# Interleaving the value matmuls of two attention branches in opposite column halves of TensorE

## What is computed

```
w    = softmax(where(key <= query, q k^T * scale, -inf));        o_mla = w v
z    = sq sk^T * scale;  log_1m = where(key < query, log_sigmoid(-z), 0)
a    = where(key < query, exp(log_sigmoid(z) + suffix_sum(log_1m)), 0);   o_sb = a sv
merged = g_mla * (o_mla @ w_branch_mla) + g_sb * (o_sb @ w_branch_sb)
```

## Time and profile before

| | |
|---|---|
| median of 3 runs | 2427.37 us (2427.21 to 2428.22) |
| profiled execution | 2424.88 us, span 2423.6 us, mean granted clock of TensorE 0.976 |
| TensorE busy | 2349.8 us, 97% of the span |
| VectorE busy | 839.4 us, 35% |
| ScalarE busy | 448.4 us, 19% |
| GpSimd busy | 1287.7 us, 53% |
| attention loop | about 1770 to 1902 us after the span's start |

### The profile page before, as it was taken

The page is one execution under the profiler, slowest core; times in us unless marked ns, Lnnn a source line. Parts: engine busy times, 40 slices in busy tenths (PEclk is TensorE's granted clock), DMA queues, the critical chain, the costliest instruction groups (busy, mean ns, idle before and its releaser), DMA issues.

```text
span 2423.6 us, 26205 instructions
## 1 busy us (share of the span) xinstructions
PE 2349.8 (97%) x11108; PEld 1938.4 (80%) x11108; DVE 839.4 (35%) x910; ACT 448.4 (19%) x712; POOL 1287.7 (53%) x734
## 2 busy tenths in 40 slices
PE   7999999999989999999999999999899999999999
PEld 6888888787768888888888888778667788888887
DVE  2323103666444333203232202430568733333013
ACT  2111003222313111003111102011257221111012
POOL 4666665754015666665666665666100456666654
PEclk9999999999679999999999999999899999999999
DMA  4333332221002333332333332233100222333322
GB/s 155 97 99 100 96 96 78 81 76 61 9 27 87 96 96 96 96 97 77 96 97 100 99 96 80 87 96 98 35 1 1 62 91 92 96 96 96 106 87 86
DMA packets 55580, 201.06 MB, mean 83 GB/s; under 512 B 6408, under 2 KB 6536, under 8 KB 55336
## 3 DMA queue, kind: packets, MB, share of 16 engines
q1 hardware_dynamic: 53712, 193.62, 25.8%
q10 hardware_dynamic: 1752, 5.77, 0.6%
HBM read 197.27 MB, written 2.10 MB: 82 GB/s over the span
## 4 chain that ended last, share of the span: by engine, by line
PE 69%; DVE 4%; ACT 1%; issue 1%; POOL 0%; DMA 0%; DVEq 0%; POOLq 0%; ACTq 0%
PE psum L340 13%; PE psum L341 13%; PE psum L342 13%; PE psum L402 6%; PE psum L400 6%; PE psum L401 6%; PE psum L478 2%; PE psum L813 1%; PE psum L821 1%; PE psum L850 1%; PE psum L592 1%; PE psum L438 1%; PE psum L959 1%; PE psum L960 1%; PE psum L961 1%
## 5 line engine op out<-in xcount | busy, mean ns | idle before, releaser
L322 POOL TENSOR_SCALAR w_hi<-w_raw 128x1024 fp32r<-128x1024 f32 (+1 forms) x365 | 396.6, 1087 | 1089.0 <-PE psum L342 583.6
L324 POOL TENSOR_TENSOR w_lo<-w_raw,w_hi 128x1024 fp32r<-128x1024 f32 (+1 forms) x365 | 891.7, 2443 | 30.5
L340 PE MATMUL psum<-u_hi,w_hi 128*128 128x512 f32 (+1 forms) x2072 | 791.3, 382 | 11.1 <-DVE work L1527 4.0
L341 PE MATMUL psum<-u_hi,w_lo 128*128 128x512 f32 (+1 forms) x2072 | 787.5, 380 | 0.0
L342 PE MATMUL psum<-u_lo,w_hi 128*128 128x512 f32 (+1 forms) x2072 | 787.0, 380 | 0.0
L340 PEld LDWEIGHTS psum<-u_hi,w_hi 128*128 128x128 f32 x2072 | 390.7, 189 | 87.9 <-DVE work L1527 4.5
L342 PEld LDWEIGHTS psum<-u_lo,w_hi 128*128 128x128 f32 x2072 | 390.7, 189 | 74.2
L341 PEld LDWEIGHTS psum<-u_hi,w_lo 128*128 128x128 f32 x2072 | 390.7, 189 | 73.1 <-issue 0.5
L400 PE MATMUL psum<-w_hi,hidden_hi 128*128 128x512 f32 x768 | 298.8, 389 | 0.0
L401 PE MATMUL psum<-w_lo,hidden_hi 128*128 128x512 f32 x768 | 298.8, 389 | 0.0
L402 PE MATMUL psum<-w_hi,hidden_lo 128*128 128x512 f32 x768 | 298.8, 389 | 0.0
(11 more groups left out here) (261 smaller groups left out, 1776.7 us busy)
## 6 DMA issues: line engine op xcount, KB each, us to landing
w_raw<-in_ffn_in SPq DMA_DIRECT2D x176, 512.0 KB, 3.5
w_raw<-in_ffn_out SPq DMA_DIRECT2D x88, 512.0 KB, 3.5
w_raw<-in_proj_in SPq DMA_DIRECT2D x34, 512.0 KB, 3.5
w_raw<-in_mix_in SPq DMA_DIRECT2D x29, 512.0 KB, 3.4
w_raw<-in_embed SPq DMA_DIRECT2D x10, 512.0 KB, 3.5
w_raw<-in_mix_out SPq DMA_DIRECT2D x8, 512.0 KB, 3.5
w_raw<-in_branch SPq DMA_DIRECT2D x8, 512.0 KB, 3.6
w_raw<-in_proj_out SPq DMA_DIRECT2D x8, 512.0 KB, 3.5
```

Source lines behind the costliest of these rows:

```text
L322: pool.tensor_scalar(hi, raw, 1.0, 1.0, ALU.mult, ALU.mult).then_inc(k.w_split, 1)
L324: pool.tensor_tensor(lo, raw, hi.bitcast(F32), ALU.subtract).then_inc(k.w_split, 1)
L340: pe.matmul(out, hi[:, cols], xhi, start=first, stop=False)
L341: pe.matmul(out, lo[:, cols], xhi, start=False, stop=False)
```

## The change

The two value steps become one function, values(h, m), which issues for each of the seven causal blocks the stick branch's matmul of head h and then the softmax branch's matmul of head m. It is called with m = h-1 relative to its stick head, so the two write opposite halves of the array's columns. In step h of TensorE's loop this is values(h-1, h-2); step 1 has the stick branch alone, and after the loop come values(7, 6) and values(None, 7).

So that head h-1's transposed probabilities can lie while those of h-2 are read, turned writes to one of two buffers by the head's parity; the odd one is in two pieces, so odd heads have two copies (1024 and 256 columns) where there was one. On VectorE mla_out(h-2) now stands behind stick_out(h-1) and ahead of softplus(h); mla_out(h-1) behind softplus(h) is gone. After the loop it runs mla_out(6) and mla_out(7) behind stick_out(7). maxima waits for the first query block's logits and, ahead of the second reduction, for the rest. The pairs are made at other steps, and the merge's first product takes the stick branch's four inputs first.

```
+        self.turned = [[(0, N_CAUSAL, turned)], [(0, 2 * T, k.big[:, 4 * T:6 * T]), (2 * T, N_CAUSAL, k.diag[:, 0:N_CAUSAL - 2 * T])]]
-COMPLETE = {1: [0], 3: [1], 4: [4], 5: [2, 5], 6: [6], 7: [3, 7]}
+COMPLETE = {3: [0], 4: [4], 5: [1, 5], 6: [6], 7: [2], 8: [7, 3]}
 pe_attend, logits:
-        m.then_inc(k.logits_done, 1)
+            if i in (ROWS[0][0], ROWS[-1][0]):
+                m.then_inc(k.logits_done, 1)
 pe_attend, values (in place of stick_values and mla_values):
+    def values(h, m):
+        if h is not None:
+            pe.wait_ge(k.z_weights, h + 1)
+            if h:
+                pe.wait_ge(k.z_out, h)
+        if m is not None:
+            pe.wait_ge(k.p_copied, m + 1)
+            if m:
+                pe.wait_ge(k.o_out, m)
+            else:
+                pe.wait_ge(k.norm_var, NORM["heads"])
+        last = len(CAUSAL_BLOCKS) - 1
+        for n, (i, t0, width, c) in enumerate(CAUSAL_BLOCKS):
+            if h is not None:
+                v = H.sv[...]
+                z = pe.matmul(k.ps[7][half(h), t0:t0 + width], v, H.z[h % 2][:, c:c + width], ...)
+            if m is not None:
+                v = H.v[...]
+                o = pe.matmul(k.ps[6][half(m), t0:t0 + width], v, H.turned_at(m, c, width), ...)
+        if h is not None:
+            z.then_inc(k.z_values, 1)
+        if m is not None:
+            o.then_inc(k.o_values, 1)
 pe_attend, loop and end:
-            stick_values(h - 1)
-            mla_values(h - 1)
+            values(h - 1, h - 2 if h > 1 else None)
...
-    stick_values(AH - 1)
-    mla_values(AH - 1)
+    values(AH - 1, AH - 2)
+    values(None, AH - 1)
 pe_merge:
-        for part in range(2):
+        for part in (1, 0):
 act_attend and dve_attend: pairs(h - 1) becomes pairs(h); ScalarE's waits for both outputs become
+            if n < 4:
+                act.wait_ge(k.o_out, 2 * n + 2)
+            else:
+                act.wait_ge(k.z_out, 2 * n - 6)
 dve_attend, maxima:
-        dve.wait_ge(k.logits_done, h + 1)
-        for i, c in ROWS:
+        dve.wait_ge(k.logits_done, 2 * h + 1)
+        for n, (i, c) in enumerate(ROWS):
+            if n == 1:
+                dve.wait_ge(k.logits_done, 2 * h + 2)
 dve_attend, turned:
-        if h:
-            dve.wait_ge(k.o_values, h)
-        dve.tensor_copy(H.turned, k.psum[:, B0:B0 + N_CAUSAL]).then_inc(k.p_copied, 1)
+        if h >= 2:
+            dve.wait_ge(k.o_values, h - 1)
+        for a, b, x in H.turned[h % 2]:
+            d = dve.tensor_copy(x[:, 0:b - a], k.psum[:, B0 + a:B0 + b])
+        d.then_inc(k.p_copied, 1)
 dve_attend, loop and end:
             stick_out(h - 1)
+            if h > 1:
+                mla_out(h - 2)
         softplus(h)
-        if h:
-            mla_out(h - 1)
...
     stick_out(AH - 1)
+    mla_out(AH - 2)
     mla_out(AH - 1)
```

More of the change, by code:

```diff
@@ L781, in __init__ @@
         self.sq, self.sk = [tile(k.big, 6 + n) for n in range(4)], [tile(k.big, 10 + n) for n in range(4)]
-        self.probs, self.turned, *self.z = (row(k.big[:, (KF + LATENT_AT) * T:], n) for n in range(4))
+        self.probs, turned, *self.z = (row(k.big[:, (KF + LATENT_AT) * T:], n) for n in range(4))
+        self.turned = [[(0, N_CAUSAL, turned)], [(0, 2 * T, k.big[:, 4 * T:6 * T]), (2 * T, N_CAUSAL, k.diag[:, 0:N_CAUSAL - 2 * T])]]
         self.soft = [row(k.scf, n) for n in range(2)]
@@ L794, in __init__, with turned_at @@
         self.o = self.sk + self.sq
-COMPLETE = {1: [0], 3: [1], 4: [4], 5: [2, 5], 6: [6], 7: [3, 7]}
+    def turned_at(self, h, c, n):
+        return next(x[:, c - a:c - a + n] for a, b, x in self.turned[h % 2] if a <= c and c + n <= b)
+COMPLETE = {3: [0], 4: [4], 5: [1, 5], 6: [6], 7: [2], 8: [7, 3]}
 PAIRS = [n for h in sorted(COMPLETE) for n in COMPLETE[h]]
+CAUSAL_BLOCKS = sorted(CAUSAL, key=lambda x: (x[0], x[1]))
 def pe_attend(k):
@@ L861, in transpose @@
         m.then_inc(k.p_turned, 1)
-    def stick_values(h):
-        pe.wait_ge(k.z_weights, h + 1)
-        if h:
[L866 to L871, removed]
-        if h:
[L873 to L877, removed]
+    def values(h, m):
[12 more added lines that the diff above has]
+            if h is not None:
+                v = H.sv[:, ((h // 2) * NT + i) * P + h % 2 * HV:((h // 2) * NT + i) * P + (h % 2 + 1) * HV]
+                z = pe.matmul(k.ps[7][half(h), t0:t0 + width], v, H.z[h % 2][:, c:c + width], start=n == 0, stop=n == last, skip_group_check=True)
+            if m is not None:
+                v = H.v[:, (m * NT + i) * HV:(m * NT + i + 1) * HV]
+                o = pe.matmul(k.ps[6][half(m), t0:t0 + width], v, H.turned_at(m, c, width), start=n == 0, stop=n == last, skip_group_check=True)
+        if h is not None:
+            z.then_inc(k.z_values, 1)
+        if m is not None:
+            o.then_inc(k.o_values, 1)
     def spread_key(h):
@@ L1341, in pairs @@
         for n in COMPLETE.get(h, ()):
-            act.wait_ge(k.o_out, h + 1)
-            act.wait_ge(k.z_out, h + 1)
+            if n < 4:
+                act.wait_ge(k.o_out, 2 * n + 2)
+            else:
+                act.wait_ge(k.z_out, 2 * n - 6)
             act.copy(tile(k.uhi, n), H.o[n]).then_inc(k.pair_hi, 1)
@@ L1358, in act_attend @@
         act.copy(H.soft_hi, s).then_inc(k.soft_hi, 1)
-        pairs(h - 1)
+        pairs(h)
     weigh(AH - 1)
-    pairs(AH - 1)
+    pairs(AH)
 def act_embed(k):
@@ L1976, in dve_attend @@
             stick_out(h - 1)
+            if h > 1:
+                mla_out(h - 2)
         softplus(h)
-        if h:
-            mla_out(h - 1)
-        else:
+        if h == 0:
             for n in range(1, AH):
```

## The result

The changed kernel takes 2444.6 us (median of 4 runs, 2443.19 to 2450.55) against 2427.29 of the kernel before: ratio 1.0079, interval 1.0059 to 1.0100. The forecast was slower by 6.8 us, 2434.2, with a range to 2446. The direction and the ring were right; the size was not: 17.3 us. That 2444.6 lies inside the range is luck: the range's upper part was kept for column halves that overlap badly (rival 1), and they overlap fully.

A forecast was written before the change was run, and what follows sets the result against it. TensorE's queue was taken as the bound, with a ring through VectorE and ScalarE 0.2 us under it. Six rings 3.4 - step 1's 0.1 + tail 1.4 + 7d, d = 0.3, gave +6.8 on 2427.37: 2434.2 us, range 2428 to 2446.

The forecast's parts named there:

- the ring: Attention loop, split to split through mask matmul, logits, transposes, values, stick_out, softplus and cast: 13.43 us without TensorE's own queue.
- rival 1: Paired values: column halves overlap badly, d from 0.5 to 2.2 us, making the kernel 9.3 to 20.1 us slower; chance 0.24.
- TensorE's queue and the ring lie 0.2 us apart: Attention loop: TensorE's queue repeats every 13.64 us, the ring takes 13.43, so freeing TensorE alone gives at most about 0.2.
- mla_out's slot: VectorE, between stick_out and softplus: the copy's new place adds 0.72 us to the ring in each head.
- Ring after, 14.15 + d: Split to split in steps 2 to 7 after the change: 14.2 + d on average against 13.64, six rings costing 3.4 + 6d.
- Step 1, 13.5 against 13.64: Loop's first step, without softmax half or mla_out: 13.5 us against 13.64, a gain of 0.1 us.
- d = 0.3: Paired values: d is the delay of the last stick pass, hence of stick_out; taken as 0.3 us, ends 0 and 2.2.
- Early maxima worth nothing: VectorE's first maxima reduction, about 0.7 us, moves earlier, but stick_out still waits for the values: counted as zero.
- Tail 1.4 + d, stall gone: Last split to merge: 11.0 + d against 9.6 us, 1.4 + d longer, with the merge's 0.38 us stall gone.
- Rival 4: TensorE's clock falls after the new waits; a fall over one head would make about +10 us; chance 0.02.

The follow-up runs named there:

- e3_busy: The changed kernel with mla_out moved back behind softplus and matmuls of constants in TensorE's waits: 2425.91 us, ratio 1.0002 to the kernel before.
- e6_unpaired_act: The kernel before, values unpaired, with the first maxima reduction ahead of the remaining logits and stick_out moved to ScalarE: 2422.3 us, ratio 0.9982.
- e8_busy_loop: The changed kernel with matmuls of constants in TensorE's waits ahead of the sums alone: 2431.13 us, ratio 1.0021 to the kernel before.
- experiment 4: The changed kernel with mla_out moved back behind softplus: 2438.8 us, ratio 1.0052; with matmuls of constants in TensorE's waits too, 2425.91 us, ratio 1.0002.
- experiment 5: The kernel before with only the first maxima reduction run ahead of the wait for the remaining logits: 2426.46 us, ratio 0.9999.
- e1_busy: The changed kernel with matmuls of constants ahead of the sums and of the last transposes and last seven value blocks: 2431.88 us, ratio 1.0026.

## Why the prediction was wrong in size

- *TensorE's queue and the ring lie 0.2 us apart; freeing TensorE alone gives nothing*: right in what it gives. e3_busy, which has the pairing without mla_out's slot and with TensorE kept busy, is 1.0002 times the kernel before. The 13.64 us are not TensorE's work alone, though: TensorE's row of weight loads shows that in the kernel before the softmax values wait 0.2 us for the copy turned, which the merged row of 28 passes hides.

```profile
1859.56 0.41 PEld L478 LDWEIGHTS psum<-work 128*64 128x64 f32 x4 [0.21 <-DVE work L1929]
```

  So 28 passes in one half after the other take 4.48 us, not 4.67, and in e6_unpaired_act, where that wait is gone, the queue repeats every 13.47 to 13.48 us.
- *Ring after, 14.15 + d*: right, 14.13 to 14.38 where the clock held (e8_busy_loop). *Step 1, 13.5 against 13.64*: wrong by little; the first two splits are 14.84 us apart before and 14.83 after, so there was no 0.1 to gain.
- *d = 0.3*: too high; it is 0. Column halves in alternation lose nothing, where the row halves of the earlier trace rows, changed every eight passes, reached 80%. That took 2.1 us from the sum. The estimate of d = 0.5 from the figure in the Trainium skill's page "TensorE: Matmul & The Clock Gate", Part 3, was too high in the same way. That part also says that tiles of the array work on several matmuls at once; the trace agrees, with starts 0.00 to 0.01 us apart.
- *mla_out's slot, 0.72 a head*: right (experiment 4). *Early maxima worth nothing*: right (experiment 5). *Tail 1.4 + d, stall gone*: right, 1.5.
- *Rival 4, the clock: "with waits of 1.94 and less it stays at 1.00 ... so it stays"*: this is the step that failed. It put the cost of the new waits at nothing. In six of the seven heads I had their lengths nearly right: up to 0.6 us on the exponents and 1.9 on the cast were forecast, and the trace has 0.50 and 1.31 to 2.17. The last head's I had wrong: "the longest I expect is some 2 us", and it is 5.12, since the 1.94 us of the earlier trace rows and the new slack add up there. From one wait of 1.94 us, behind 96 us in which TensorE had no pause (1793 to 1889 us), I concluded that any number of such waits is free. The trace of the kernel before spoke against that already: at the start of the attention loop the clock fell within a microsecond of a wait of 0.52 us (the row behind the wait, then two windows with the granted clock).

```profile
1770.15 3.90 PE L813 MATMUL psum<-work 64*128 64x128 f32 x14 [0.52 <-DVE work L1882]
...
1769.00:1771.00 2.00, 1.49 (x14) 1.33 (x14) 1.43 (x5) 1.85 (x3) 0.00 (x0) 1.00 0.00 0
1771.00:1777.00 6.00, 6.00 (x13) 3.00 (x12) 2.26 (x5) 3.67 (x4) 0.00 (x0) 0.50 0.00 1
```

  What the runs showed in its place: the clock fell in all seven heads of the profile. The mask matmul came 2.5 to 3.4 us after the split's end rather than 1.4, which is 11.3 us in the seven heads, and the logits behind it took another 2.8 us in four of them. In the medians the clock's cost is the difference between the changed kernel and the two with TensorE kept busy in full: 17.3 less 5.0 to 6.5, so 11 to 12 us, nearly twice what the forecast had for the whole change. I gave it 0.02, and a price of 10 us for one head; in this profile a fall costs 1.2 to 2.8 us, but it came seven times.

What exactly makes the clock fall stays open: not the length of the gap ahead of it (1.31 us and it fell, 1.45 and it held once and fell twice, 1.94 and it held), and one fall was seen in e1_busy's profile with a gap of 0.7 us only. The runs show that fewer and shorter pauses make falls rare, no more.

## What to carry to other kernels

Before taking work off TensorE in a loop where another ring through VectorE and ScalarE is as long, work out how long TensorE will then wait in each turn, and price its passes behind that wait at the lower clock as well; shorten that ring first (here one copy moved to ScalarE and one back behind softplus turned +17 us into -9, and another order of the last heads into -12). What stands between a wait and the ring's next step costs its full time, even if it is 0.7 us that was free in its old place.

## What the runs showed of the hardware that I had not expected

- Matmuls of 64 columns that alternate between the two column halves start in pairs, 0.01 us apart, and 28 float32 passes take no longer than 14 in one half (stick_out is released after 2.42 us in both). Issued as two groups, they hardly overlap (4.1 us).
- The granted clock fell to 0.50 in each of seven heads, with pauses of 1.3 to 2.2 us ahead of the sums (5.1 in the last), and stayed there for 3.4 to 6.8 us. With dummy matmuls in the pauses it did not fall in one profile (e8_busy_loop) and fell once in another (e1_busy).
- The same unchanged stage differed by some 6 us between two executions, by how long the clock stayed at 0.50 in it.
